# Start of a two-model block kernel: order of the first loads, of the pool weights and of the pool mixer's products

## The reference, cut to what matters

```
h = rms_norm(x, norm_mix[0])                 # per token: x / sqrt(mean(x^2) + eps), times a gain per column
for g, win in enumerate((2, 4, 8, 16)):      # four groups of 256 columns
    mean = (sum of h over the last win tokens) / min(tokens so far, win)
    p[:, :, g] = mean - h[:, :, g]
y = einsum('bsgc,gcd->bsgd', p, w)           # four 256x256 products
x = x + y * scale                            # a scale per output column
```

## Time and profile before

| | us |
|---|---|
| median of 3 runs | 900.47 (899.12 to 900.85) |
| profiled execution, whole | 899.84 |
| its span, first to last instruction | 897.7 |
| PE busy | 881.1 (98%) |
| DVE, ACT, GpSimd busy | 674.1, 479.1, 54.4 |
| first transpose after the pool mixer (line 1845) starts | 23.34 |

### The profile page before, as it was taken

How to read it: one execution, slowest core, us unless ns; L and a number is a source line. 1 busy time by engine, 2 the same in 40 slices (tenths; PEclk the granted TensorE clock), 3 DMA queues, 4 the chain that set the end, 5 groups by cost and what they waited for, 6 DMA issues and landing times.

```text
span 897.7 us, 14482 instructions
## 1 busy us (share of the span) xinstructions
PE 881.1 (98%) x5258; PEld 780.7 (87%) x5258; DVE 674.1 (75%) x1015; ACT 479.1 (53%) x750; POOL 54.4 (6%) x91
## 2 busy tenths in 40 slices
PE   9999999999999999999999999999999899999996
PEld 7888888889998888888888999997998788888885
DVE  5887767777646588677667788896644799999997
ACT  6744444456565665344444645455544665556554
POOL 3300000020000000000000510001100000000000
PEclk9999999999999999999999999999999999999999
DMA  8986666552532768566546784312544566676631
GB/s 254 317 235 192 203 180 179 164 175 84 165 141 94 216 174 252 179 187 207 179 132 207 177 240 156 104 48 71 186 169 115 165 187 184 192 210 186 175 108 47
DMA packets 185574, 153.47 MB, mean 171 GB/s; under 512 B 5089, under 2 KB 170593, under 8 KB 185522
## 3 DMA queue, kind: packets, MB, share of 16 engines
q1 hardware_dynamic: 184770, 150.36, 55.1%
q0 software_dynamic: 752, 2.39, 1.0%
HBM read 151.17 MB, written 1.05 MB: 170 GB/s over the span
## 4 chain that ended last, share of the span: by engine, by line
PE 65%; DVE 21%; issue 5%; ACT 5%; DMA 1%; DVEq 1%; SPq 0%; POOL 0%; POOLq 0%; ACTq 0%
PE bank L1973 17%; PE bank L1828 10%; PE bank L1830 10%; PE bank L1829 10%; PE bank L1979 9%; DVE wl L1221 3%; DVE cu L1187 2%; DVE wl L1082 2%; DVE us L1176 2%; ACT wh L588 2%; DVE cg L1187 2%; DVE gs L1170 1%; DVE dl L1213 1%; PE bank L1845 1%; PE bank L1944 1%
## 5 line engine op out<-in xcount | busy, mean ns | idle before, releaser
L1973 PE MATMUL bank<-xhl,wh 128*128 128x512 f32 x1008 | 240.3, 390 | 0.0
L1973 PEld LDWEIGHTS bank<-xhl,wh 128*128 128x128 f32 x1008 | 188.8, 188 | 41.0 <-issue 0.3
L1979 PEld LDWEIGHTS bank<-xhl,wl 128*128 128x128 f32 x1008 | 129.2, 191 | 4.9
L1979 PE MATMUL bank<-xhl,wl 128*128 128x256 f32 x1008 | 130.7, 283 | 0.0
L1221 DVE TENSOR_TENSOR wl<-raw,wh 128x2048 fp32r<-128x2048 f32 x57 | 130.1, 2282 | 0.2 <-ACT wh L674 0.2
L1082 DVE TENSOR_TENSOR wl<-raw,wh 128x2048 fp32r<-128x2048 f32 (+3 forms) x50 | 104.2, 2095 | 28.4 <-ACT wh L588 28.3
L674 ACT ACTIVATE wh<-raw 128x2048 fp32r<-128x2048 f32 x57 | 108.7, 1907 | 1.9 <-DMA raw<-in_ffn_w_up 1.7
L1828 PE MATMUL bank<-dh,hh 128*128 128x512 f32 x264 | 102.9, 390 | 0.5 <-DVE hl L1206 0.5
L1830 PE MATMUL bank<-dh,hl 128*128 128x512 f32 x264 | 103.4, 392 | 0.0
L1829 PE MATMUL bank<-dl,hh 128*128 128x512 f32 x264 | 103.1, 390 | 0.0
L588 ACT ACTIVATE wh<-raw 128x2048 fp32r<-128x2048 f32 (+3 forms) x51 | 89.6, 1769 | 17.6 <-PE bank L1830 7.1
(11 more groups left out here) (331 smaller groups left out, 1549.9 us busy)
## 6 DMA issues: line engine op xcount, KB each, us to landing
raw<-in_ffn_w_up SPq DMA_DIRECT2D x88, 512.0 KB, 6.1
draw<-in_ffn_w_down SPq DMA_DIRECT2D x66, 512.0 KB, 3.5
raw<-in_ffn_w_gate SPq DMA_DIRECT2D x44, 512.0 KB, 5.3
raw<-in_w_in SPq DMA_DIRECT2D x16, 512.0 KB, 5.1
raw<-in_mla_w_o SPq DMA_DIRECT2D x8, 512.0 KB, 3.7
raw<-in_xattn_wv SPq DMA_DIRECT2D x8, 512.0 KB, 4.7
raw<-in_w_out SPq DMA_DIRECT2D x8, 512.0 KB, 4.0
raw<-in_xattn_wq SPq DMA_DIRECT2D x8, 512.0 KB, 4.6
```

Source lines behind the costliest of these rows:

```text
L1973: pe.matmul(banks[half][:, :].rearrange("p (a s) -> p a s", a=2), wh[ns][:, a:a + P], xhl[:, :, k, :], start=k == 0, stop=False, skip_grou ...
L1979: ins = pe.matmul(banks[half][:, 0:SEQ], wl[ns][:, a:a + P], xh[:, k, :], start=False, stop=k == KD - 1, skip_group_check=True)
```

## The change

It has six parts. The loads: both x tiles first, then the bands in two halves (groups 0 and 1, groups 2 and 3, the host lays them out so), then pool weights half 0, the gain columns, pool weights half 1; the pool scale is now issued by GpSimd as its first instruction. The squares of x are one instruction of 1024 columns for each tile and not two of 512. The scaled bands are made in halves, two for x0 and two (each an edge and a body) for x1, and PE waits for a half before the four blocks that use it. PE has three more products on zeros (`WARM_BAND`) between the spreading of the scale and the band products. DVE does pool weights half 0, then the low parts of blocks 0 and 1, then pool weights half 1, then blocks 2 and 3. In the last pool products PE does high by high for both tiles, low by high for both, high by low for both.

```diff
-WARM_PRODUCTS, WARM_POOL, WARM_BETWEEN = 8, 3, 3
+WARM_PRODUCTS, WARM_BAND, WARM_POOL, WARM_BETWEEN = 8, 3, 3, 3
+BAND_HALF = NBAND // 2
...
             for t in range(NT):
                 sp.dma_start(xt[:, t, :], x_dram[:, t, :]).then_inc(x_tile[t], 16)
-                if t == 0:
-                    sp.dma_start(band[:, :], bands).then_inc(band_loaded, 16)
-                    sp.dma_start(pscale[:, :], w["pool_scale"][0:1, :]).then_inc(pscale_loaded, 16)
-            sp.dma_start(col[:, :], columns_in).then_inc(col_loaded, 16)
+            for half in range(2):
+                part = slice(half * BAND_HALF, (half + 1) * BAND_HALF)
+                sp.dma_start(band[:, part], bands[:, part]).then_inc(band_loaded[half], 16)
             for i, (v, (ks, cs_), src) in enumerate(blocks[0][2]):
                 sp.dma_start(v(raw[0])[:, ks, cs_], src).then_inc(pool_part[i], 16)
+                if i == 0:
+                    sp.dma_start(col[:, :], columns_in).then_inc(col_loaded, 16)
...
+            for t in range(NT):
+                act.wait_ge(x_tile[t], 16)
+                if t:
+                    act.wait_ge(sq_done, 2 * t)
+                act.activation(gain[:, :], xt[:, t, :], ACT.Square, scale=ROOT_D, accum_out=ss[:, 0, t, 0:1]) \
+                   .then_inc(sq_done, 2)
...
             for half in range(2):
                 split_t(0, xh, C_MIX0, 0, range(2 * half, 2 * half + 2), 2 * half)
-                act.wait_ge(pool_scaled, 3 + half)
+                act.wait_ge(pool_scaled, 2 * NT + half + 1)
...
-            dve.wait_ge(band_loaded, 16)
             dve.wait_ge(rstd_done, 1)
-            dve.tensor_scalar(bandr[:, 0:FRONT], band[:, 0:FRONT], rstd[:, 0, 0:1], None, ALU.mult).then_inc(pool_scaled, 1)
+            for half in range(2):
+                dve.wait_ge(band_loaded[half], 16)
+                dve.tensor_scalar(bandr[:, half * FRONT // 2:(half + 1) * FRONT // 2], front(half), rstd[:, 0, 0:1], None,
+                                  ALU.mult).then_inc(pool_scaled, 1)
...
                 dve.tensor_tensor(rv[:, gs_, :, :], rv[:, gs_, :, :], pv_, ALU.mult).then_inc(pool_scaled, 1)
-            dve.wait_ge(col_loaded, 16)
-            split_t(0, xh, xl, C_MIX0, 0, range(4))
+                if half == 0:
+                    dve.wait_ge(col_loaded, 16)
+                split_t(0, xh, xl, C_MIX0, 0, range(2 * half, 2 * half + 2), 2 * half)
...
+            pool.dma_start(pscale[:, :], w["pool_scale"][0:1, :]).then_inc(pscale_loaded, 16)
             then(pool.memset(mhalf[:, :], -0.5))
...
+            for _ in range(WARM_BAND):
+                pe.matmul(bank[5][:, 0:SEQ], zeros[:, 0:P], zeros, start=True, stop=True)
             for t in range(NT):
                 pe.wait_ge(x_tile[t], 16)
-                pe.wait_ge(pool_scaled, t + 1)
                 for k in range(KD):
+                    if k % 4 == 0:
+                        pe.wait_ge(pool_scaled, 2 * t + k // 4 + 1)
...
             for t in range(NT):
                 pool_pass(1, t, xh, h_, True)
-                if t == 0:
-                    pe.wait_ge(t_lo, 8)
+            pe.wait_ge(t_lo, 8)
+            for t in range(NT):
                 pool_pass(1, t, xl, h_)
-                if t == 0:
-                    pe.wait_ge(lo_done, 1)
+            pe.wait_ge(lo_done, 1)
+            for t in range(NT):
                 pool_pass(1, t, xh, l_).then_inc((bank_sum, block_used)[t], 1)
```

More of the change, by code:

```diff
@@ L139, in constants @@
             full[g, tok, tok] -= 1.0
-    bands[:, :FRONT] = full[:, :P, :P + EDGE].transpose(1, 0, 2).reshape(P, -1)
-    bands[:, FRONT:] = full[:, P:, P:P + EDGE].transpose(1, 0, 2).reshape(P, -1)
+    for half in range(2):
+        gs_ = slice(2 * half, 2 * half + 2)
+        b = half * BAND_HALF
+        bands[:, b:b + FRONT // 2] = full[gs_, :P, :P + EDGE].transpose(1, 0, 2).reshape(P, -1)
+        bands[:, b + FRONT // 2:b + BAND_HALF] = full[gs_, P:, P:P + EDGE].transpose(1, 0, 2).reshape(P, -1)
     assert np.array_equal(full[:, P:, P + EDGE:], full[:, :P, EDGE:P])
@@ L401, in build @@
         pool_part, pool_hi, pool_lo = [sem("pool_part0"), sem("pool_part1")], sem("pool_hi"), sem("pool_lo")
-        con_loaded, band_loaded = sem("con_loaded"), sem("band_loaded")
+        con_loaded, band_loaded = sem("con_loaded"), [sem("band_loaded0"), sem("band_loaded1")]
         mem_loaded, pscale_loaded = sem("mem_loaded"), sem("pscale_loaded")
@@ L723, in square @@
                                scale=ROOT_D, accum_out=ss[:, q, t, c:c + 1]).then_inc(sq_done, 1)
[L725 to L728, removed]
             act.wait_ge(col_loaded, 16)
@@ L1260, in by_group, with front @@
             def by_group(ap):
-                return ap.rearrange("p (g c) -> p g c", g=NG)
-            dve.wait_ge(band_loaded, 16)
+                return ap.rearrange("p (g c) -> p g c", g=NG // 2)
+            def front(half):
+                return band[:, half * BAND_HALF:half * BAND_HALF + FRONT // 2]
             dve.wait_ge(rstd_done, 1)
-            dve.tensor_scalar(bandr[:, 0:FRONT], band[:, 0:FRONT], rstd[:, 0, 0:1], None, ALU.mult).then_inc(pool_scaled, 1)
+            for half in range(2):
+                dve.wait_ge(band_loaded[half], 16)
+                dve.tensor_scalar(bandr[:, half * FRONT // 2:(half + 1) * FRONT // 2], front(half), rstd[:, 0, 0:1], None,
+                                  ALU.mult).then_inc(pool_scaled, 1)
             dve.wait_ge(rstd_done, 2)
[L1268 to L1271, removed]
+            for half in range(2):
+                second_tile = by_group(bandr[:, FRONT + half * 2 * P:FRONT + (half + 1) * 2 * P])
+                edge = band[:, half * BAND_HALF + FRONT // 2:(half + 1) * BAND_HALF]
+                dve.tensor_scalar(second_tile[:, :, 0:EDGE], by_group(edge), rstd[:, 0, 1:2], None, ALU.mult)
+                dve.tensor_scalar(second_tile[:, :, EDGE:P], by_group(front(half))[:, :, EDGE:P], rstd[:, 0, 1:2], None,
+                                  ALU.mult).then_inc(pool_scaled, 1)
             dve.wait_ge(scale_spread, 1)
@@ L1738, in inverse_rms_after_norm @@
                     pool.tensor_tensor(rstd[:, 6, one], st2[:, 6, one], r, ALU.mult).then_inc(rstd_done, 1)
+            pool.dma_start(pscale[:, :], w["pool_scale"][0:1, :]).then_inc(pscale_loaded, 16)
             then(pool.memset(mhalf[:, :], -0.5))
             pool.memset(ksw[:, :, :, :], 0.0).then_inc(ksw_zero, 1)
-            inverse_rms(0)
+            for t in range(NT):
+                one = slice(t, t + 1)
+                pool.wait_ge(sq_done, 2 * t + 2)
+                then(pool.tensor_scalar(st1[:, 0, one], ss[:, 0, t, 0:1], EPS, None, ALU.add))
+                pool.tensor_tensor(rstd[:, 0, one], st1[:, 0, one], mhalf[:, 0:1], ALU.pow).then_inc(rstd_done, 1)
             pool.wait_ge(hi_done, 1)
```

## The result

The changed kernel is slower: 902.11 us against 899.69 us (medians of 15 runs each), ratio 1.0022 with a 95% interval of 1.0014 to 1.0029, so 1.3 to 2.6 us. The profiled execution took 901.68 us with a span of 899.3, against 899.84 and 897.7. The forecast was 901.5 with a range of 899.7 to 903.0. Its direction, its mechanism and its range held. Its size did not: it said +1.05 us, and the ratio gives 2.0 (the medians differ by 2.4), with only the lower edge of the interval inside its likeliest band of +0.7 to +1.4. The time of 901.5 came within 0.6 us of 902.11 partly by luck.

A forecast was written before the change was run, and what follows sets the result against it. PE, 98% busy, was taken as the bound, so a delay of its first transpose counts in full: 0.36 us from PE's later end plus 0.7 from product order, +1.05, giving 901.5 us against the median; range 899.7 to 903.0.

The forecast's parts named there:

- x first: Loads at the start: x1 lands at 6.6 us and not 7.94; its branch gains about 1.5 us, ending at PE's queue.
- Warm products: PE ahead of the x0 band products: three added products take 1.1 us, upper bound 1.46, and nothing hides them.
- Pool scale by GpSimd: Small load on GpSimd's queue at the start: issued at 0.8, lands at 5.3, needed at 6.47, so costs nothing.
- Rival B: Pool scale lands late and PE waits for it: +2.4 us (902.9), or +4.5 (905) by the slower row; chance 0.15.
- DVE's new order: DVE at the pool weights: idles 2.1 us before blocks 0 and 1; adds start at 18.7, 0.55 us late.
- Order of the last products: End of PE's pool products: the third add comes late, so the new order makes the last add 0.7 us later.
- Rival C: Reordering the last pool products costs only 0 to 0.2 us, total +0.4 (900.9); chance 0.18, shared with near no change.
- The sum: First transpose behind the pool mixer starts at 24.4 and not 23.34, 1.05 us late; profiled execution 900.9, median 901.5.
- Rival A: PE's early warm records run faster as the clock rises sooner, up to 1.75 us gained: -0.7 us, 899.8; chance 0.17.

The follow-up runs named there:

- a_bands_first: Changed kernel with the loads of x1 and the bands exchanged (x0, both band halves, x1); ratio 1.0028 to the kernel before.
- a_no_warm_band: Changed kernel without the three warm products ahead of the band products; ratio 1.0010 to the kernel before.
- a_warm_band6: Changed kernel with six warm products ahead of the bands and not three; ratio 1.0043 to the kernel before.
- c_warm6: Changed kernel without warm products ahead of the bands, with DVE's and the last products' old orders, and six warm products at the start, not eight; ratio 1.0003.
- a_old_dve: Changed kernel with DVE's old order (both pool weight halves, then low parts of blocks 0 to 3); ratio 1.0025 to the kernel before.
- b_new_products: Kernel before with only the last pool products put in the new order; ratio 1.0009 to the kernel before.
- a_old_products: Changed kernel with the last pool products in the old order (all three kinds for tile 0, then tile 1); ratio 1.0023.
- a_quarter_late: Changed kernel with DVE making the second quarter of the feed-forward weights' low part behind the fourth add, not between third and fourth; ratio 1.0039.
- b_warm_band: Kernel before with only three warm products added ahead of its band products; ratio 1.0016 to the kernel before.

## Why the prediction was right, and where its size was off

**x first.** x1 was forecast at 6.6 and was there by 5.9, the x1 bands at about 9.5 and were ready by 8.6; too cautious both, and without effect, as a_bands_first shows. That the gain ends at PE's queue was right.

**Warm products.** Forecast 1.1 from a row whose last product overlaps the next in the trace; measured 1.40 in the timeline and 1.29 to 1.31 in T - S (a_no_warm_band, a_warm_band6). The upper bound of 1.46 was nearer than the value taken. What followed was taken too long by almost as much: from the start of the bands to ACT's first pair the forecast counts 2.07 + 0.78 = 2.85, and with no wait for x1 it was 2.66 (10.13 to 12.79).

**Pool scale by GpSimd.** Forecast 5.3, measured 6.0, hidden at S = 6.8. Rival B did not occur. Issued as first instruction it started at 1.33 and not 0.8, and the small load alone took 4.7 us, not less than one of 512 KB. Its margin ahead of the spreading was thus 0.8 us in the changed kernel, and none in c_warm6.

**DVE's new order.** DVE idled 3.5 us and not 2.1; the price was right in kind and 0.3 in size (a_old_dve).

**Order of the last products.** The forecast put 0.7 behind PE's last product, and 0.73 is what b_new_products shows there. But it is not what the order costs: 0.36 of it comes back because PE ends sooner, and what is left is 0.37 in either kernel (a_old_products, b_new_products). Rival C's 0 to 0.2 was too little. The reason was half right: the late third add, yes; the quarter and the fourth add queued behind it, no, since the path over GpSimd's rms factor is as long (a_quarter_late).

**The sum.** Forecast T = 24.4 at S = 6.47, which is S + 17.93; measured S + 17.96. The two terms that were off, the warm products by 0.3 and the way from the bands to ACT's first pair by 0.2, went opposite ways and nearly cancelled. What was mis-sized is the difference from the kernel before. It was worked out for one execution, the one in which S was 6.47. But S is not a constant. In the thirteen profiles with eight warm products at the start it lay between 6.47 and 7.97, mean 7.17, and that of before was the lowest of them. The kernel before absorbs a late S up to 7.36; the changed one passes on each tenth. An estimate, which takes those thirteen values of S for both kernels: the changed kernel's T is 7.17 + 17.96 = 25.1 in the mean, and that of before (the later of S + 15.98 and 23.34) 23.5, so 1.7 us. With x1's bands as early as in b_new_products, which would put 22.97 in place of 23.34, it is 1.9. The ratios are 1.0018 to 1.0021, inside 1.0014 to 1.0029. That the spread of S makes up the difference is thus worked out and fits; the timed executions do not show their S.

**Rival A.** The prediction had the very fact there: that the early warm records run slow and that the moment at which the clock rises sets S. It drew only the faster side from it, as a chance of the changed kernel, and not that it moves both kernels and one of them more. Its price was wrong besides. A gain of 1.75 needs S = 4.7, and the prediction's own landing of the pool scale, 5.3, forbids that; in ten of the eleven profiles with that load on GpSimd's queue it landed at 5.8 or later. So the lower end of the range, 899.7, had nothing under it.

**Behind T.** The rest of the span lay between 873.3 and 875.9 in all profiles, with a granted clock of 0.994 to 0.999, and not in the order of the ratios. In b_warm_band, b_new_products and a_bands_first the clock was 0.83 to 0.85 in the stretch from 590 to 600 us, where that of before and of the changed kernel was 1.00. Such dips need no edit: in its own timed runs beside these variants the kernel before had a granted clock of 0.994 to 0.999, and its spans were 897.3 in the mean at 0.998 or more and 898.6 at 0.996 or less. What brings them was not looked into.

## What to carry to other kernels

A transfer that ends last in the chain of waits is worth moving only as far as the reserve of the engine behind it: PE was 0.9 us or less from being the bound, so once filler was added to its queue, x1's data came two microseconds earlier and gained nothing, and what the filler took beyond that reserve came on top. Read a stretch relative to an event inside it (here T - S) when the start is noisy: it separated effects of 0.3 us that five rounds of timing could not. The event must lie behind the last thing that varies, though: in b_new_products x1's landing varied too, and T - S misled until the reading began behind the band products. And where one profile shows a start-up time, ask whether both versions react to it alike, since a kernel with slack hides a spread that one without it shows in full.

## What the runs showed of the hardware that was not expected

- The same sixteen warm records took 5.2 to 6.7 us (5.20 in the kernel before, 6.70 in a_no_warm_band), with no difference in PE's code ahead of them. The early ones last 0.63 us and the later ones 0.38, and how many are slow changes from run to run: they are slow until about 4.3 us in the kernel before, and until about 7.3 in a_no_warm_band. The granted clock in the profile reads 1.00 over this stretch, so it does not show it; the durations do.
- The clock stayed at its upper level behind the spreading products (1.9 us on a single row) in thirteen profiles with eight warm products ahead, and fell there in the one with six. The Trainium skill (TensorE: Matmul & The Clock Gate, HAM oscillation) warns of gaps in which PE is idle; here the idle time was 0.31 us, and the kernel before kept its clock over gaps of 0.65 and 0.94.
- A 4 KB load alone on GpSimd's queue took 3.6 to 4.9 us from issue to landing in eleven profiles. The Trainium skill (DMA: Bandwidth & Descriptors, Anatomy of one DMA) gives an estimate of 2.0. The traces do not agree, at least beside SyncE's large loads, which ran in all of them.
